# Two steps a block in place of three for the linear attentions of a hybrid mixer, and a new order of VectorE's first steps

## The reference, cut to what matters

```
o_mla = block_causal_attention(q_mla, k_mla, v)        # 8 latent heads, softmax, 64 nope + 32 rope
o_gla = rms(gla_chunked(q, k, v, log_a)) * silu(gr)    # 4 gated heads, chunks of 64
o_ret = rms(retention_chunked(q, k, v)) * silu(rg)     # 4 retention heads, chunks of 64
return concatenate([o_mla, o_gla, o_ret]) @ w_out
```

## Time and profile before

| what | value |
|---|---|
| median of 3 runs | 1931.03 us (1926.86 to 1933.93) |
| the profiled execution | 1929.26 us, its span 1927.5 us |
| TensorE busy | 1897.9 us of the span |
| VectorE, ScalarE, GpSimd busy | 1223.5, 803.7, 652.8 us |
| the loop of layer 0, layer 1 | about 476 to 578 us, 1428 to 1530 us |
| mean granted TensorE clock | 0.996 |

### The profile page before, as it was taken

How to read it: one execution, slowest core, us unless ns; L and a number is a source line. 1 busy time by engine, 2 the same in 40 slices (tenths; PEclk the granted TensorE clock), 3 DMA queues, 4 the chain that set the end, 5 groups by cost and what they waited for, 6 DMA issues and landing times.

```text
span 1927.5 us, 31402 instructions
## 1 busy us (share of the span) xinstructions
PE 1897.9 (98%) x12876; PEld 1694.6 (88%) x12876; DVE 1223.5 (63%) x1609; ACT 803.7 (42%) x1160; POOL 652.8 (34%) x498
## 2 busy tenths in 40 slices
PE   8999999999999999999999999999999999999998
PEld 7999988897568999998899999889956789999886
DVE  6888843534555788872578888344354567888523
ACT  5344433324564443442344444233345544444322
POOL 3666500002231566610046663000022325666000
PEclk9999999999999999999999999999999999999999
DMA  4232233221013122233312223332200212322321
GB/s 155 88 109 109 103 124 123 96 109 44 1 47 108 66 107 90 109 127 113 131 45 91 107 109 111 130 135 93 87 22 2 97 68 78 109 102 94 131 99 66
DMA packets 27228, 179.97 MB, mean 93 GB/s; under 512 B 3283, under 2 KB 3445, under 8 KB 7158
## 3 DMA queue, kind: packets, MB, share of 16 engines
q1 hardware_dynamic: 25618, 173.63, 24.9%
q10 hardware_dynamic: 1508, 4.94, 0.7%
HBM read 176.45 MB, written 2.10 MB: 93 GB/s over the span
## 4 chain that ended last, share of the span: by engine, by line
PE 94%; DVE 2%; ACT 2%; issue 1%; POOL 1%; DMA 0%; SPq 0%; POOLq 0%; DVEq 0%; ACTq 0%
PE ps L485 27%; PE ps L487 27%; PE ps L486 27%; PE ps L865 2%; PE ps L746 1%; PE ps L497 1%; PE ps L884 1%; PE ps L664 1%; PE ps L666 1%; PE ps L665 1%; PE ps L872 1%; PE ps L782 1%; PE ps L802 0%; PE ps L808 0%; PE ps L899 0%
## 5 line engine op out<-in xcount | busy, mean ns | idle before, releaser
L485 PE MATMUL ps<-xH,WH 128*128 128x256 f32 (+2 forms) x1408 | 421.2, 299 | 0.7 <-DVE WL L1474 0.5
L487 PE MATMUL ps<-xH,WL 128*128 128x256 f32 (+2 forms) x1408 | 418.7, 297 | 0.0
L486 PE MATMUL ps<-xL,WH 128*128 128x256 f32 (+2 forms) x1408 | 418.6, 297 | 0.0
L485 PE MATMUL ps<-TH,WH 128*128 128x256 f32 x1216 | 344.1, 283 | 0.0
L486 PE MATMUL ps<-TL,WH 128*128 128x256 f32 x1216 | 344.1, 283 | 0.0
L487 PE MATMUL ps<-TH,WL 128*128 128x256 f32 x1216 | 344.1, 283 | 0.0
L1352 DVE TENSOR_TENSOR WL<-raw,WH 128x2048 fp32r<-128x2048 f32 x62 | 143.1, 2309 | 262.2 <-ACT WH L987 249.6
L485 PEld LDWEIGHTS ps<-xH,WH 128*128 128x128 f32 (+1 forms) x1408 | 268.9, 191 | 9.5 <-issue 2.1
L486 PEld LDWEIGHTS ps<-xL,WH 128*128 128x128 f32 (+1 forms) x1408 | 268.8, 191 | 8.5 <-issue 1.0
L487 PEld LDWEIGHTS ps<-xH,WL 128*128 128x128 f32 (+1 forms) x1408 | 268.8, 191 | 7.6
L485 PEld LDWEIGHTS ps<-TH,WH 128*128 128x128 f32 x1216 | 233.5, 192 | 0.0
(11 more groups left out here) (272 smaller groups left out, 3671.4 us busy)
## 6 DMA issues: line engine op xcount, KB each, us to landing
raw<-stream SPq DMA_DIRECT2D x156, 1024.0 KB, 4.8
norm_g<-norm_gains SPq DMA_DIRECT2D x11, 512.0 KB, 5.2
x<-x_in SPq DMA_DIRECT2D x4, 512.0 KB, 7.1
wq<-w_q_up ACTq DMA_DIRECT2D x4, 512.0 KB
out<-x SPq DMA_DIRECT2D x4, 512.0 KB, 2.6
const<-consts ACTq DMA_DIRECT2D x2, 610.5 KB
wkv<-w_kv_up ACTq DMA_DIRECT2D x2, 512.0 KB
cos<-positions ACTq DMA_DIRECT2D x2, 256.0 KB
```

The costliest lines, as they stand in the source:

```text
L485: mm(dst, wh, xh, start=start, stop=False)
L486: mm(dst, wh, xl, start=False, stop=False)
L487: return mm(dst, wl, xh, start=False, stop=stop)
```

## The change

What it does, by part:

- The linear attentions take two steps a block: `PARTS` = 2. linear_scores(b) is in the first and linear_values(b) in the second; VectorE does decayed(b) and keep_low(b) both in the first.
- `LIN_STEP` = 2: state_parts(1) and add_states(1) move ahead of the loop (on TensorE between scores(0) and scores(1), on VectorE behind tops(0)), and steps 0 and 1 have parts 2 and 3. In these steps TensorE does them ahead of make_q, and VectorE ahead of turn_q.
- NORM_STEP becomes 10 and GATE_STEP 15 by this, on all engines.
- turn_q(h) no longer waits for keep_q(h).
- At stage 0 VectorE does normed(0, 0) ahead of average_x(0, 1).

```diff
-LIN_STEP = 3
-PARTS = 3
+LIN_STEP = 2
+PARTS = 2
@@ TensorE
                         if n < LIN_STEP:
-                            state_parts(n + 1)
+                            state_parts(n + 2)
@@
                     scores(0)
+                    state_parts(1)
                     scores(1)
                     scores(2)
                     for n in range(STEPS):
@@
                         if n and n % 2 == 0:
                             values(n // 2 - 1)
+                        if n < LIN_STEP:
+                            linear(n)
                         if i < HEADS // 2:
@@
                         if n % 8 == 7:
                             spread_shares(i - 1)
-                        linear(n)
+                        if n >= LIN_STEP:
+                            linear(n)
@@ VectorE
                         average_x(0, 0)
+                        normed(0, 0)
                         average_x(0, 1)
-                        normed(0, 0)
                         normed(0, 1)
@@ turn_q
-                        dve.wait_ge(q_kept, due(q_kept, h + 1))
@@
                         if n < LIN_STEP:
-                            add_states(n + 1)
+                            add_states(n + 2)
                         elif n < NORM_STEP:
                             b, part = divmod(n - LIN_STEP, PARTS)
                             if part == 0:
                                 decayed(b)
-                            elif part == 1:
                                 keep_low(b)
@@
-                    for m in range(AHEAD):
-                        tops(m)
+                    tops(0)
+                    add_states(1)
+                    tops(1)
+                    tops(2)
                     for n in range(STEPS):
@@
+                        ready = n < LIN_STEP or n < NORM_STEP and (n - LIN_STEP) % PARTS == 1
+                        if ready:
+                            linear(n)
                         if i < HEADS // 2 and n % 8 in (0, 4):
                             turn_q(2 * i + n % 8 // 4)
-                        linear(n)
+                        if not ready:
+                            linear(n)
```

## The result

| kernel | median us | range | ratio to before, 95% interval |
|---|---|---|---|
| before | 1928.9 | 1926.4 to 1933.9 (6 runs) | |
| after | 1939.6 | 1937.7 to 1941.5 (6 runs) | 1.0059 [1.0048, 1.0071] |

The change makes the kernel 10.6 us slower. The forecast was 1936, some 5.6 us slower; the time lies inside the range, but the loss is nearly twice the forecast one. It stands between rival 1 (the sum, +5.6) and rival 2 (the sum and further clock stretches, +12.4), and just beyond the 0.5% within which I put "same".

A forecast was written before the change was run, and what follows sets the result against it. TensorE, busy 98% of the span, bounds the kernel, so only its waits matter. +3.0 a layer, +6.0 for both, less 0.4 at the start, gives +5.6 on the median 1931.0: 1936, range 1929 to 1943.

The forecast's parts named there:

- rival 1: Whole kernel: the sum of terms holds as it stands, 3 to 9 us slower, 1932 to 1940; chance 0.60.
- rival 2: Steps 3 to 20: new waits bring two further slow-clock stretches a layer, 1.7 us each, +12.4, 1943; chance 0.12.
- First steps: Loop start: waits for turn_q(1) and state_parts(3) go, state_parts(2) waits a new 0.8; -2.2 us a layer.
- keep_q and turn_q at once: ScalarE and VectorE in different halves of one PSUM bank: nothing added; if served in turn, scores(1) waits some 0.15 us.
- The blocks: Two steps a block: TensorE waits 0.8, 0.5, 1.2, 1.1 on the 1.9 us copy chain; net +2.0 a layer.
- Squares and power: linear_squares(0) waits 0.9 for ScalarE's squares, linear_spread(0) 0.9 for GpSimd's power, both moved five steps earlier.
- The gate: Step 17: ScalarE waits 2.7 us for GpSimd's gated tile; TensorE waits 0.4 and 1.4; net +1.35 a layer.
- The step that failed: Earlier low_half of output weights on VectorE and high(9) on ScalarE, 1.2 and 1.9 us: cost nothing.
- the clock: One fall to 1.2 GHz per layer's loop, 3.4 us at half, counted the same in both kernels as ScalarE paced it.
- Rival 3: Step 17: GpSimd and ScalarE don't meet, 1.8 us a layer less, +2.0, 1933; chance 0.12.
- Rival 4: Block chain is hidden, its 3.6 us a layer don't appear on top, -1.6, 1929.4; chance 0.13.
- The start of the program: normed(0,0) ahead of average_x(0,1) brings everything to the first dense pair 0.4 us earlier, bounds 0 and 0.8.

The follow-up runs named there:

- e7: Changed kernel with VectorE's copy of the lower scores (keep_low) done twice, one behind the other, same result; 1952.6 us, ratio to before 1.0125.
- e5: Changed kernel with only the split of the output weights moved back to steps 29 and 30; 1937.5 us, ratio to before 1.0047.
- e2: Changed kernel with squares, gate and weight split back at the steps of before (15, 20, 29), still two steps a block; 1925.4 us, ratio 0.9994.
- e4: Changed kernel with VectorE's reciprocal of the share totals put ahead of linear(n); 1936.9 us, ratio to before 1.0039.
- e3: Changed kernel with gate and weight split back at steps 20 and 29, squares staying at 10; 1932.0 us, ratio to before 1.0019.
- e8: Changed kernel with three steps a block again, squares at step 14, gate at 20, weight split at 29; 1919.1 us, ratio to before 0.9952.
- e10: Changed kernel with squares, gate and split at 15, 20, 29 and the reciprocal ahead of linear(n); 1930.6 us, ratio to before 1.0003.
- e1: Changed kernel with three steps a block again, so squares from step 14 and gate from 19; 1924.1 us, ratio to before 0.998.

## Why the prediction was right, and where it fell short

The direction, the mechanism and most terms held, but the sum is nearly half too small: forecast was +3.0 a layer, and the loop grew by 5.5. That the time itself is only 3.6 us off is in part luck, since the forecast stood on 1931.0 for before, of which six executions give 1928.9. Term by term:

- **First steps.** Forecast -2.2. state_parts(2) waits 0.88 (forecast 0.8), state_parts(3) doesn't, and the waits for qT are gone. One wait grew: state_parts of the first steps, for ScalarE's kT, 0.75 in place of 0.25 a layer. From the lists: 1.65 now; before 1.5 + 1.3 + 0.45 (make_k on qT) + 0.25 + 0.2 = 3.7; so -2.05.
- **keep_q and turn_q at once.** In the changed trace ScalarE and VectorE read the two halves of one PSUM bank together:

```profile
484.75 0.59 ACT L1216 ACTIVATE qT<-ps 64x512 f32<-64x512 f32 x1 [2.14 <-PE ps L746]
...
484.82 0.68 DVE L1651 TENSOR_TENSOR qT<-ps,cos 64x512 f32<-64x512 f32 x1 [0.32 <-PE ps L746]
```

  turn_q takes 0.68 as in the earlier trace rows, where it ran alone, and keep_q 0.59 as in before. By the Trainium skill (PSUM — Partial Sum Buffer, the section on bank collisions) two engines may be in different quadrants of one bank at the same time; this trace agrees.
- **The blocks.** Forecast 0.8, 0.5, 1.2, 1.1; measured 0.92, 0.61, 1.28, 1.25, so 4.1 in place of 3.6. e7 shows that the chain paces them. The upper copy, the lower copy and the reciprocal of block 2 (each with the idle time before it):

```profile
512.93 0.77 ACT L1270 ACTIVATE attn_g<-ps 64x256 f32<-64x256 f32 x2 [1.17 <-PE ps L782]
...
513.84 0.89 DVE L1680 COPY_PREDICATED attn_g<-const,ps 64x256 f32<-64x256 int32 x2 [0.48 <-issue]
...
514.76 0.20 DVE L1743 RECIPROCAL share<-total 128x8 f32<-128x8 f32 x1
```

  From the start of the upper copy to the end of the reciprocal are 2.03 us. By my terms 0.77 + 0.05 + 0.90 + 0.2 = 1.92. The missing 0.1 is in the hand-over from ScalarE to VectorE, 0.14 where I took 0.05, and it is by about this that each of the four waits is over its forecast.
- **Squares and power.** 1.09 and 1.16 (forecast 0.9 and 0.9).
- **The gate.** The meeting in step 17 is as forecast. On the left the start; GpSimd's low part and first gating, then ScalarE:

```profile
556.00 1.28 POOL L1901 TENSOR_TENSOR xL<-kt_ret,xH 128x512 fp32r<-128x512 f32 x1 [8.60 <-ACT xH L1248]
...
557.24 1.26 POOL L1918 TENSOR_TENSOR heads<-heads,gate 128x512 f32<-128x512 f32 x1
...
558.54 0.63 ACT L1286 ACTIVATE xH<-heads 128x512 fp32r<-128x512 f32 x1 [2.62 <-POOL heads L1918]
```

  ScalarE stood still 2.62 (forecast 2.7), TensorE waited 1.26 at values(9) (forecast 1.4). The 0.4 at scores(22) didn't show.
- **The step that failed: "They cost 1.2 and 1.9 us on engines with room there ... Cost nothing."** VectorE has room on average, but each half of the split went ahead of a row maximum that ScalarE wanted at once. TensorE's waits from step 26 on are 0.47 + 0.35 + 0.22 = 1.04, where I had the 0.45 of before going away. Without the early split (e5) the loop is 1.6 shorter, so this is the largest single miss.

The waits together are 10.3 - 5.7 = +4.6 a layer in place of 3.0: the split +1.0, the blocks +0.5, squares and power +0.45, the start +0.15, less 0.55 at the gate, 1.55 by these and 1.6 by the lists. The miss at the gate goes the other way and hides a part of the rest. The other 0.9 of the 5.5 isn't in the list of waits.

It isn't **the clock** either, which I had counted equal. The same pieces can be held against a kernel whose loop has no stretch. From the second squares to make_q(7), first before, then e2; from the first squares to the second, first the changed kernel, then layer 0 of e4 (same columns as the windows above):

```profile
542.82:551.22 8.40, 8.40 (x45) 5.05 (x43) 3.80 (x13) 6.66 (x15) 6.24 (x2) 0.80 0.37 128
```

```profile
543.84:550.65 6.81, 6.81 (x46) 4.50 (x44) 3.26 (x12) 6.29 (x15) 4.66 (x1) 1.00 0.42 158
```

```profile
532.59:539.81 7.22, 7.22 (x33) 4.45 (x34) 1.76 (x4) 3.82 (x9) 0.00 (x0) 0.76 0.41 145
```

```profile
528.69:534.27 5.58, 5.58 (x33) 3.76 (x34) 1.76 (x4) 3.84 (x9) 0.00 (x0) 1.00 0.51 188
```

The stretch costs 1.6 us in both places. So the count was right and its reason wrong: the piece that I took to be paced by ScalarE covered nothing.

The 0.9 is in pieces during which TensorE is on record as busy: 97.26 us in the loop of before, 98.16 in that of the changed kernel (windows of 103.00 and 108.40 us). At least that much hangs on the moved tail, as the whole loop's busy time falls from 98.4 (changed) by 0.6 with the split back (e5), by a further 0.65 with the gate back too (e3), and by a further 0.3 beyond the stretch with the squares back (e2). The first steps may add to it; they weren't compared for this. What lengthens the pieces isn't shown.

**The rivals.** Rival 1, the sum, is what happened, mis-sized: +10.6 in place of +5.6. Rival 2's price is right (1.65 measured, 1.7 forecast), but the changed kernel drew no further stretch in its loops. e7 shows that it can happen, with waits of up to 2.2 us: two further stretches a layer. The Trainium skill (TensorE: Matmul & The Clock Gate, Part 1) ties the clock to idle time, and the rows agree in direction at most: e8, idle for 2.2 us a loop, has no stretch, after (10.3) has one, e7 (13.9) three; but before with 5.7 has one and e2 with 6.2 none, and at 9.1 e4 has none in one layer and two in the other, as has e10 at 4.95. Rival 3 fell (ScalarE did wait 2.62). Rival 4 fell by e7: the waits grow with the chain.

The start of the program moved the first matmul of a projection from 414.53 to 414.36, 0.2 earlier in place of 0.4. The other kernels with the same start have it anywhere from 413.6 to 414.5, on average 414.1. TensorE's wait for xn there is 1.5 us in all of them and 2.3 in before. This fits the 0.4, but there is one trace of before only, and the term wasn't tested alone.

Open: what decides whether a stretch at 1.2 GHz falls in a loop. The same program has one in layer 0 and none in layer 1 (e1), or two and none (e10). The squares don't decide it alone: in before, the changed kernel and e3 the stretch begins within 1.5 us of the end of squares, but in e1 it comes 6 us behind them, and e2 and e8 have the same squares and no stretch.

## What to carry to other kernels

When a loop that interleaves two computations is made shorter, cost what comes after it as carefully as the shortened part: here the tail that moved with the counter was worth more (7.2 us a layer back in e2) than the two steps a block (3.9), and taking the new order's good half with the tail left in place (e8) beat before by 0.5% and the changed kernel by 1%. An engine with 37% of its time free can still delay the bound one, if a long instruction goes ahead of a short one that others wait for; look at what stands behind each moved instruction, not at busy shares. Where TensorE is the bound, reckon a wait at its length, and count a clock stretch of 1.6 us on top as possible, not as given. Where executions of one kernel differ in their stretches, one trace doesn't show the usual case; look at the mean granted clock of all of them.

## What the runs showed of the hardware

- The granted clock falls for 3.4 us at a time (or 6.8), to 0.5, and one such stretch costs 1.65 us over dense matmuls. No wait of TensorE in these loops is longer than 2.2 us, and stretches fall all the same, none to three in a loop of 100 to 115 us. The most waiting (e7, 13.9 us a loop) has the most and the least (e8, 2.2) none; between them the order doesn't hold (e4 at 9.1 has none in one layer). In e7 lengthening four waits of about 1 to about 2 us brought two more.
- By this, a wait can cost nearly twice its length: e7 added 3.65 us of waits a layer and 6.8 us of time.
- The same program doesn't draw the same stretches in every execution, and some kernels spread much more by it than others: e10 1922.8 to 1932.0 us at a mean clock of 0.997 to 0.992 (12 executions), e8 1918.0 to 1919.4 at 0.997 (5).
- ScalarE and VectorE read two halves of one PSUM bank at the same time, in 0.59 and 0.68 us, both as when alone.
